# A two-layer RWKV-7 / HGRN2 decoder step: projections and recurrence in one program, with gated rows and two output weights kept on the chip

## What is computed

```python
    proj = jnp.einsum('btnd,nde->btne', xs[:, :, :4], w_in)
    r, k, v, z = proj[:, :, 0], proj[:, :, 1], proj[:, :, 2], proj[:, :, 3]
    w_log = -jax.nn.softplus(-(w0 + jnp.tanh(xw @ w1) @ w2)) - 0.5
    a = jax.nn.sigmoid(a0 + (xa @ a1) @ a2)
    ...
    def step(S, inp):
        r_t, w_t, k_t, v_t, kk_t, b_t = inp
        sa = jnp.einsum('bhvk,bhk->bhv', S, -kk_t)
        S = S * w_t[:, :, None, :] + sa[..., None] * b_t[:, :, None, :] + v_t[..., None] * k_t[:, :, None, :]
        return S, jnp.einsum('bhvk,bhk->bhv', S, r_t)
    ...
    out = (y.astype(x.dtype) * jax.nn.silu(z)) @ w_o
```

## Time and profile before

| | |
|---|---|
| median of 3 runs | 2975.45 us (2975.07 to 2979.83) |
| the profiled execution, its own time | 2976.09 us |
| its span in the trace | 2974.3 us |
| PE busy | 2799.4 us, 94% of the span |
| DVE busy | 1330.3 us, 45% |
| ACT busy | 1128.1 us, 38% |
| mean granted TensorE clock | 0.979 of full speed |

### The profile page before, as it was taken

The page is one execution under the profiler, slowest core; times in us unless marked ns, Lnnn a source line. Parts: engine busy times, 40 slices in busy tenths (PEclk is TensorE's granted clock), DMA queues, the critical chain, the costliest instruction groups (busy, mean ns, idle before and its releaser), DMA issues. The chain is left out here.

```text
span 2974.3 us, 81376 instructions
## 1 busy us (share of the span) xinstructions
PE 2799.4 (94%) x37104; PEld 2632.9 (89%) x37104; DVE 1330.3 (45%) x2185; ACT 1128.1 (38%) x1560; POOL 106.7 (4%) x91
## 2 busy tenths in 40 slices
PE   5999999999978999999869989999999999999995
PEld 4899999999967888788769979999999999998995
DVE  4434313322117777788632264434444344444223
ACT  5444323322225555555432253333333333333321
POOL 0000000000000000000000000000000000000000
PEclk8999999999989999999989999999999999999998
DMA  3233333333311111221152232222222222222322
GB/s 121 86 106 110 116 108 112 108 114 117 108 66 52 59 59 59 59 60 58 41 196 94 86 133 87 83 84 95 87 87 80 87 95 87 87 77 84 116 86 97
DMA packets 81926, 271.18 MB, mean 91 GB/s; under 512 B 16176, under 2 KB 22064, under 8 KB 61104
## 3 DMA queue, kind: packets, MB, share of 16 engines
q1 hardware_dynamic: 72368, 248.14, 24.7%
q10 hardware_dynamic: 9216, 17.83, 1.6%
HBM read 220.51 MB, written 45.42 MB: 89 GB/s over the span
## 5 line engine op out<-in xcount | busy, mean ns | idle before, releaser
L114 PE MATMUL t_pair<-t_x_hi,t_w_hi 128*128 128x272 f32 x3072 | 674.3, 301 | 39.9 <-DVE t_x_lo L1635 30.2
L114 PE MATMUL t_pair<-t_x_hi,t_w_lo 128*128 128x272 f32 x3072 | 638.8, 290 | 0.0
L114 PE MATMUL t_pair<-t_x_lo,t_w_hi 128*128 128x272 f32 x3072 | 637.9, 289 | 0.0
L114 PEld LDWEIGHTS t_pair<-t_x_hi,t_w_hi 128*128 128x128 f32 x3072 | 483.9, 190 | 71.6 <-issue 44.3
L114 PEld LDWEIGHTS t_pair<-t_x_lo,t_w_hi 128*128 128x128 f32 x3072 | 486.4, 190 | 0.0
L114 PEld LDWEIGHTS t_pair<-t_x_hi,t_w_lo 128*128 128x128 f32 x3072 | 483.8, 190 | 0.0
L114 PE MATMUL ab_pair<-ab_x_hi,ab_w_hi 128*128 128x272 f32 x2048 | 433.4, 293 | 23.9 <-ACT ab_x_hi L283 19.2
L114 PE MATMUL ab_pair<-ab_x_hi,ab_w_lo 128*128 128x272 f32 x2048 | 426.1, 290 | 0.0
L114 PE MATMUL ab_pair<-ab_x_lo,ab_w_hi 128*128 128x272 f32 x2048 | 424.8, 289 | 0.0
L326 DVE TENSOR_TENSOR ab_w_lo<-ab_raw,ab_w_hi 128x2048 fp32r<-128x2048 f32 x64 | 146.6, 2293 | 524.1 <-ACT ab_w_hi L258 524.1
L114 PEld LDWEIGHTS ab_pair<-ab_x_hi,ab_w_hi 128*128 128x128 f32 x2048 | 326.2, 190 | 29.6 <-issue 21.0
(11 more groups left out here) (332 smaller groups left out, 3632.3 us busy)
## 6 DMA issues: line engine op xcount, KB each, us to landing
ab_raw<-in_w_in SPq DMA_DIRECT2D x64, 1024.0 KB, 4.9
t_raw<-in_hgrn_in SPq DMA_DIRECT2D x64, 1024.0 KB, 4.9
t_raw<-in_rwkv_wo SPq DMA_DIRECT2D x16, 1024.0 KB, 4.8
t_raw<-in_hgrn_wo SPq DMA_DIRECT2D x16, 1024.0 KB, 4.9
t_Ss<-in_hgrn_s SPq DMA_DIRECT2D x16, 512.0 KB, 4.5
out_hgrn_s<-t_Sd SPq DMA_DIRECT2D x16, 512.0 KB, 6.7
ab_nxt<-in_x SPq DMA_DIRECT2D x4, 1088.0 KB, 9.1
scr_r<-ab_stage ACTq DMA_DIRECT2D x16, 272.0 KB, 2.1
```

The lines of the kernel that those rows point to most:

```text
L114: mm = pe.matmul(out[:, a, 0:TH], w, x[:, kt, a * TH:(a + 1) * TH], start=(kt == 0 and n == 0), stop=(kt == KT - 1 and n == 2))
```

## The change

`rwkv_dense` and `rwkv_recurrence` become one block, `rwkv`. The work that passes `i = -2` and `i = -1` did, the front of pair 0, is taken apart and put between the steps of the z tiles 51 to 63 by one function `first_pair` for each engine: on PE at a given tile and step, on ACT and DVE in the pass over tile n - 1, behind that pass's evacuation and weight split, on SP behind the load of weight n. The loop begins at `i = 0`. In the doubling levels of pair 0 the products go to another PSUM bank (`c1_ps`), since the usual one belongs to the tiles. The buffers of the recurrence are laid over those of the projections (`Area`). The product `yc * zs` is written to `o`, which stays on the chip into `trunk`, with the weight buffers and their high and low parts. In pass 13 SP loads the first two output weights into the free weight buffers, in pass 15 ACT casts them and DVE subtracts. `trunk` starts with the casts of the 16 rows.

```diff
+def rwkv(nc, keep, d):
...
+        lora, raw, w_hi, w_lo, o = keep.lora, keep.raw, keep.w_hi, keep.w_lo, keep.o
+        area = Area(nc, "a", keep.o_at)
+        later = Area(nc, "c", keep.o_at + 4 * KT * T)
...
+        early = Area(nc, "b", area.at)
+        early_at = early.at
...
+        assert later.at <= early_at
...
+            def first_pair(n):
+                if n == 51:
+                    sp.wait_ge(p.last_ready, 2)
+                    sp.dma_start(d.last, last[:, :, :]).then_inc(p.last_out, 16)
+                    sp.wait_ge(p.x_hi_ready, NT)
+                    sp.wait_ge(p.x_lo_ready, NT)
+                    for b in range(2):
+                        sp.wait_ge(stored[b], 16 * (KT + 1))
+                    load_k(0)
+                    load_w2w(0)
+                    sp.dma_start(table[:, :], d.consts[:, col0:col1]).then_inc(s.const_in, 16)
+                    load_w2a(0)
+                    load_k(1)
+                    load_r(0)
+                    load_v(0)
+                    load_state(0)
+                elif n == 56:
+                    sp.wait_ge(s.lora_w, 1)
+                    load_w2w(1)
+                elif n == 57:
+                    sp.wait_ge(s.lora_a, 1)
+                    load_w2a(1)
+                elif n == 58:
+                    sp.wait_ge(s.ksq, 1)
+                    sp.wait_ge(s.kkn, 1)
+                    sp.wait_ge(s.k2, 1)
+                    load_k(2)
+                elif n == 59:
+                    sp.wait_ge(s.rk, 1)
+                    sp.wait_ge(s.rho, 1)
+                    load_r(1)
+                elif n == 62:
+                    sp.wait_ge(s.lora_w, 2)
+                    load_w2w(2)
+            for n in range(2, NT):
+                sp.wait_ge(p.raw_hi, n - 1)
+                sp.wait_ge(p.raw_lo, n - 1)
+                sp.dma_start(raw[n % 2][:, :], d.w_in[n]).then_inc(raw_in[n % 2], 16)
+                first_pair(n)
+                for i in LORA_AT.get(n - 3, ()):
...
                 j, h = i + 1, i + 2
-                if i >= 0:
-                    if i >= 1:
-                        sp.wait_ge(s.yz, i)
-                        sp.dma_start(d.yz[i - 1], yc[:, :]).then_inc(s.yz_out, 16)
-                    sp.dma_start(zs[:, :], d.rkvz[3][i]).then_inc(s.z_in, 16)
+                if i >= 1:
+                    sp.wait_ge(s.yz, i)
+                if i == KT - 3:
+                    sp.wait_ge(p.raw_hi, NT)
+                    sp.wait_ge(p.raw_lo, NT)
+                    for b in range(2):
+                        sp.dma_start(raw[b][:, :], d.rwkv_wo[b]).then_inc(s.o_in, 16)
+                n = (NPRJ - 1) * KT + i
+                sp.wait_ge(stored[n % 2], 16 * (n // 2 + 1))
+                sp.dma_start(zs[:, :], d.rkvz[3][i]).then_inc(s.z_in, 16)
                 if h < KT:
-                    if j >= 0:
...
+            def first_pair(n, kt):
+                if (n, kt) == (51, 2):
+                    pe.wait_ge(s.const_in, 16)
+                    pe.wait_ge(p.lora_out, 2)
+                    square_sum(0)
+                elif (n, kt) == (51, 9):
+                    rank_w(0)
+                elif (n, kt) == (52, 8):
+                    rank_a(0)
+                elif (n, kt) == (53, 12):
+                    bonus(0)
+                elif (n, kt) == (54, 12):
+                    strict(0)
+                elif (n, kt) == (55, 5):
+                    b_and_k_by_token(0)
+                elif (n, kt) == (55, 11):
+                    a_and_v_by_token(0)
+                elif (n, kt) == (56, 3):
+                    inclusive(0)
+                elif (n, kt) == (56, 6):
+                    square_sum(1)
+                elif (n, kt) == (56, 13):
+                    rank_w(1)
+                elif 57 <= n < 57 + NL and kt == 3:
+                    level_x(0, n - 56)
+                elif 57 <= n < 57 + NL and kt == 9:
+                    level_yt(0, n - 56)
+                elif (n, kt) == (63, 4):
+                    pe.wait_ge(p.evac, 63)
+                    samples(0)
+                elif (n, kt) == (63, 11):
+                    sample_right(0)
...
+            for n in range(2, NT):
+                b = n % 2
+                pe.wait_ge(p.raw_hi, n + 1)
+                pe.wait_ge(p.raw_lo, n + 1)
+                pe.wait_ge(p.evac, n - 1)
+                steps = dict(zip((7, 10, 13, 15), LORA_AT.get(n - 1, ())))
+                for kt in range(KT):
+                    if n % KT == 0:
+                        pe.wait_ge(p.x_hi_ready, n + kt + 1)
+                        pe.wait_ge(p.x_lo_ready, n + kt + 1)
+                    mm = dense_kt(pe, pair[b], w_hi[b], w_lo[b], x_hi, x_lo, kt)
+                    if kt == KT - 1:
+                        mm.then_inc(p.tile_ready, 1)
+                    elif n % KT == KT - 1 and n != NT - 1:
+                        mm.then_inc(p.kt_used, 1)
+                    if kt in steps:
+                        lora_step(steps[kt])
+                    first_pair(n, kt)
+            pe.wait_ge(p.evac, NT)
+            for i in range(KT):
...
+            def first_pair(n):
+                if n == 50:
+                    act.wait_ge(p.x_lo_ready, NT)
+                    key_square(0)
+                elif n == 51:
+                    key_root(0)
+                elif n == 52:
+                    gate_w(0)
+                elif n == 53:
+                    gate_a(0)
+                    decay_before(0)
+                elif n == 54:
+                    key_square(1)
+                    act.wait_ge(s.const_in, 16)
+                    decay_after(0)
+                elif n == 55:
+                    b_and_k_tokens(0)
+                    a_and_v_tokens(0)
+                elif n == 56:
+                    key_root(1)
+                elif n == NT - 1:
+                    sample_tokens(0)
+            for n in range(2):
...
-                    act.activation(halves(csx[:, :]), q[:, :, 0:TH], ACT.Sigmoid, bias=w0).then_inc(s.sgw, 1)
+                    gate_w(j)
+                if i == KT - 1:
+                    act.wait_ge(s.o_in, 32)
+                    for b in range(2):
+                        act.copy(w_hi[b][:, :], raw[b][:, :]).then_inc(s.o_hi, 1)
                 if back:
                     act.wait_ge(s.sR_mm, i + 1)
                     act.copy(Rs[:, :], cut(m_ps, 0)).then_inc(s.sR, 1)
                 if front:
...
+            def first_pair(n):
+                if n == 51:
+                    dve.wait_ge(p.x_hi_ready, NT)
+                    key_floor(0)
+                elif n == 52:
+                    key_unit(0)
+                    dve.wait_ge(s.const_in, 16)
+                    decay_sum(0)
+                elif n == 53:
+                    sum_before(0)
+                    key_factor(0)
+                    new_key(0)
+                    bonus_rows(0)
+                    inputs_by_decay(0)
+                elif n == 54:
+                    removal(0)
+                    bonus_out(0)
+                    dve.wait_ge(s.zeroed, 3)
+                    sample_inputs(0)
+                    decayed_r(0)
+                elif n == 55:
+                    first_inverse(0)
+                    key_matrix(0)
+                elif n == 56:
+                    removal_matrix(0)
+                    key_floor(1)
+                elif 57 <= n < 57 + NL:
+                    if n == 57:
+                        key_unit(1)
+                    mask_x(0, n - 56)
+                    if n - 56 < NL:
+                        add_tit(0, n - 56)
+                        turn_ti(0, n - 56)
...
+                if i == KT - 1:
+                    for b in range(2):
+                        dve.wait_ge(s.o_hi, b + 1)
+                        dve.tensor_tensor(w_lo[b][:, :], raw[b][:, :], w_hi[b][:, :].bitcast(F32), ALU.subtract
+                                          ).then_inc(s.o_lo, 1)
                 if back:
                     dve.wait_ge(s.rs, i + 1)
                     dve.wait_ge(s.yc, i + 1)
@@ -1060,7 +1278,11 @@
                 if back:
                     dve.wait_ge(s.yb, i + 1)
                     dve.wait_ge(s.z_in, 16 * (i + 1))
-                    dve.tensor_tensor(yc[:, :], yc[:, :], zs[:, :], ALU.mult).then_inc(s.yz, 1)
+                    if i == 0:
+                        dve.wait_ge(p.last_out, 16)
+                        for b in range(2):
+                            dve.wait_ge(stored[b], 16 * (NT // 2))
+                    dve.tensor_tensor(o[:, i, :], yc[:, :], zs[:, :], ALU.mult).then_inc(s.yz, 1)
 
 
...
             def weights(g):
-                if g >= 2:
-                    sp.wait_ge(s.raw_hi, g - 1)
-                    sp.wait_ge(s.raw_lo, g - 1)
+                if g >= 4:
+                    sp.wait_ge(s.raw_hi, g - 3)
+                    sp.wait_ge(s.raw_lo, g - 3)
                 sp.dma_start(raw[g % 2][:, :], weight_tile(g)).then_inc(raw_in[g % 2], 16)
 
 ```

(33 more changed lines are left out.)

865 lines of the change are left out of this document (438 added, 427 removed).

## The result

| | median | lowest to highest, runs | profiled execution | its span |
|---|---|---|---|---|
| before | 2975.38 us | 2975.07 to 2979.83, 4 | 2976.09 | 2974.3 |
| after | 2951.59 us | 2951.21 to 2952.23, 4 | 2951.57 | 2949.8 |

The ratio is 0.9917, 95% interval 0.9900 to 0.9934. The change gains 23.8 us where 34 were forecast, and 2951.6 lies 1.6 us outside the range of 2933 to 2950. The sign and both seams came out as argued. Most of what is missing was lost in places that the forecast had left at zero.

The account below looks back on a forecast made before the run. PE was taken to bound the kernel, losing time at two seams around the recurrence; savings of 20.5 and 14.4 us, 34.9 in all, took the 2975.45 median to 2940.5, stated as 2941, range 2933 to 2950.

Parts of the forecast that it names:

- both seams: Projections into recurrence, 54.8 us to 34.3, 20.5 saved; recurrence into output projection, 44.0 to 29.6, 14.4 saved.
- Seam two: From DVE's last recurrence product to tile 1 of the output projection done: 44.0 us before, 29.6 after, 14.4 saved.
- the low clock: Output projection's start: PE, idle some 8 us, begins at low clock and loses 2.6 us, bounds 1.5 and 3.5.
- The wait of tile 55: Tile 55, step 5: PE waits 3.5 us for `MT`, `TiT` and `Mak`; no other such wait in the tiles.
- clock: Behind tile 55's wait: 3.3 us at 0.50, half of it lost, 1.6 us, bounds 0 and 3.
- Products and restarts: Tiles 51 to 63: inserted products 22.2 us on PE, plus 2 for 16 interruptions of dense work, bounds 0 to 3.2.
- Into the loop: After tile 63: evacuation, store, table load, sigmoid, scan and last addition, so `first_right(0)` starts 5.0 us after the tile.
- the 2.66 us for a switch: ACT's table switches: the skill's cost per load and drain, against 1.28 in the row; by it 19.1 saved, not 20.5.
- All tiles behind tile 1 wait for the same things in the same order as before and should only shift: Output projection behind tile 1: no change in its time, so no term in the sum.
- The loop unchanged at 576.3: Recurrence from `first_right(0)` to DVE's last product: its time stays as before, 1496.8 - 920.5 = 576.3 us.
- The sentence that the 2 MB cost nothing: Output weights requested over 70 us ahead: only pass 13's z row stands behind them on SP's queue; cost nothing.
- rival B: More waits in the tiles, six losing about 1.3 us each, low clock at loop start: 2946 to 2951, chance 0.17.

Follow-up runs that it names:

- the gates early: Kernel after, with pair 1's gates, scan and rank product and pair 0's last inverse addition moved into tiles 58 to 62: ratio 0.9897 to the kernel before.
- The run with rows and weights in line: Kernel after, with unused tiles added so rows and weights begin at the same remainder of 2048 bytes in both blocks: median 2945.65 us, ratio 0.9893.
- the last version: Kernel after with rows and weights at equal remainders, token products later in tile 55, pair 1's gates inside tiles, output weights in pieces: 2936.84 us, ratio 0.9864.

## Why the prediction missed

- **Seam two** held: 28.85 for 29.6. Start 1.5 for 1.4, PE 1.5 later as said; the low clock cost 1.8 of the 25.88 and not 2.6.
- **The wait of tile 55** held in place, size and releaser: 3.42 for 3.5. The **clock** term came out at 3.0 and not 1.6 in the profiled execution, with 6 us at the lower level behind the wait. That is an accident of the execution in part: four other profiles show 3 us and 1.5 to 1.7, as in the earlier trace rows. The stated bound of 3 is the highest value seen.
- **Products and restarts** in the tiles: 31.6 less 6.4 leaves 25.2 for 24.2. A tile with two level products is 14.52 long, 2.4 more than tile 50 and 2.6 more than tile 62, so 1.2 to 1.3 each, where 1.03 and 0.125 were taken. That is the upper half of the 0 to 3.2 given for restarts.
- **Into the loop**: 5.3 for 5.0. It was no lower bound of the program; with the gates early it is 1.6. The sigmoid followed its table load (901.55, 1.28 long) at 902.84 with nothing between, so the 2.66 us for a switch that the prediction weighed did not show.
- **"All tiles behind tile 1 wait for the same things in the same order as before and should only shift"** is the step that failed. They do wait for the same things, but the same matmuls take another time at other addresses: 4.0 us behind tile 1 and 3.2 in tiles 3 to 50, for which there was no term at all. The run with rows and weights in line gave back 3.6 and 3.1 of them. With these 7.2 us the forecast would have been 2948, inside its range. Shown is that moving the buffers did it; which places are fast, and why a tile behind inserted products goes faster at the same place, is open.
- **The loop unchanged at 576.3** failed by 1.3, as a sum: 3.5 more in pass 13 from the 2 MB, 3.6 less in the other fourteen passes, whose stops were 4.1 shorter in this execution, 0.8 more before the first copy of `TA`, where the clock was low, and 0.7 more behind the last. The loop took 576.2 to 581.1 in the profiles of the changed kernel and its versions, so its 1.3 is no measure of the 2 MB. The sentence that the 2 MB cost nothing looked at what stands behind them on SP's queue. What shared the DMA engines with them was not in the list.
- **The rivals.** The time lies by rival B's 2946 to 2951, but not for its reasons: no second tile waits, and the table loads are covered. Its loop start at the low clock did come, and cost part of the 5.3 and the 0.8 just named. The stated range ended at 2950, 1 us short of B's own 2951.

## What to carry to other kernels

A change that moves buffers changes every instruction that reads them: compare one undisturbed unit of work (a tile, a pass) of the two traces before any theory of waits, and keep a term for it; here it was 7.2 us in some 2040 of mostly dense work. A large transfer inside a stretch of many small matmuls costs more than its queue shows; look for PE's idle time that ends in "issue", and for a packet of the instruction queue just before its end. A term for the clock behind a wait has two sizes at least, by the execution: read it from several profiles. And small products were best mixed with dense ones: alone, with a gap behind each, they ran at the lower clock.

## What the runs showed of the hardware

- The same 96 matmuls took 11.94 to 12.11 us by the place of rows and weights in SBUF, with the granted clock at 1.00. For this kernel 0.08 more a projection tile and 0.03 more an output tile, with some 0.16 a pass of HGRN2, were 7 us.
- At one and the same place they took 12.10 in an unbroken stream (tile 50) and 11.94 behind tiles with inserted products (tile 62).
- PE stops in mid-run for lack of instructions. A pass of the loop without such a stop over 0.25 takes 36.0 to 36.7 us, and most of the others are longer by about what they stopped, pass 13 by the clock besides: 9.6 us of stops in 15 passes before, 7.0 after, 9.9 in the last version. The longest that did not stand behind 2 MB was 1.51. That these are blocks of instructions arriving late is read from the traces: 185 of 200 stops end 1.2 to 1.7 us behind a packet of q8, and in all ten cases behind 2 MB of loads the packet came 7.3 to 8.0 us after the one before. No run changed that queue itself. The Trainium skill, "Runtime: NRT & Kernel Launch", Instruction fetch mechanics, says that a sequencer refills itself through its own DMA queue in blocks of 16 KiB, at a cost that is mostly hidden. The size agrees with the trace (q8: 294 packets, 4.82 MB), the hiding does not hold behind 2 MB, where PE stopped 1.9 to 3.0 us.
- With 37 of 58 us busy in products with gaps of 0.8 to 1.5 between them PE stayed at 0.51 of its clock, and a level product took 1.97; the 3.4 us gap of tile 55 was followed by 6 us at 0.50 in some profiles and by 3 us in others.
